# A router-driven expert loop on TensorE: the gate phase ahead of the down phase in each round

## The reference, cut to what matters

```python
def expert_block(args):                       # one block of up to 128 rows of one expert
    xblk, e = args
    gate = xblk @ w_gate[e] + b_gate[e]
    up = xblk @ w_up[e] + b_up[e]
    gate = jnp.minimum(gate, SWIGLU_LIMIT)
    up = jnp.clip(up, -SWIGLU_LIMIT, SWIGLU_LIMIT)
    h = (up + 1.0) * gate * jax.nn.sigmoid(SWIGLU_ALPHA * gate)
    return h @ w_down[e] + b_down[e]
```

## Time and profile before

| what | us |
|---|---|
| median of 3 runs (2397.16 to 2398.49) | 2397.28 |
| the profiled execution's own time | 2394.5 |
| its span in the profile | 2392.6 |
| TensorE matmuls busy (share of the span) | 2221.9 (93%) |
| VectorE busy | 1043.4 (44%) |
| ScalarE busy | 668.5 (28%) |
| GpSimd busy | 376.6 (16%) |

### The profile page before, as it was taken

One profiled execution on the slowest core, in us unless ns is written; L12 is line 12 of the kernel. 1 busy time (PEld: TensorE's weight loads), 2 busy tenths in 40 slices (PEclk: granted clock), 3 DMA queues, 4 the chain that ended last, 5 costly groups with the idle time before them and its releaser, 6 DMA issues.

```text
span 2392.6 us, 57077 instructions
## 1 busy us (share of the span) xinstructions
PE 2221.9 (93%) x21767; PEld 1176.8 (49%) x21768; DVE 1043.4 (44%) x1664; ACT 668.5 (28%) x1414; POOL 376.6 (16%) x491
## 2 busy tenths in 40 slices
PE   5999999998996599999999999999998999999982
PEld 3485765867454244545445454444443444444441
DVE  4154547445346344434434443443353444433334
ACT  5111222233344332222322222322232222222222
POOL 5000000000014212111111121111122112211111
PEclk9999999999997699999999999999999999999996
DMA  9112011126205294967979788888887897888864
GB/s 302 35 36 72 26 33 48 31 67 246 93 36 202 90 373 127 360 211 279 338 250 344 251 313 314 287 305 287 286 328 272 303 340 271 309 291 337 322 216 157
DMA packets 187702, 525.54 MB, mean 220 GB/s; under 512 B 20330, under 2 KB 68066, under 8 KB 187490
## 3 DMA queue, kind: packets, MB, share of 16 engines
q1 hardware_dynamic: 133874, 338.86, 37.7%
q10 hardware_dynamic: 36240, 134.29, 14.4%
q0 software_dynamic: 17536, 51.69, 9.6%
HBM read 486.21 MB, written 38.57 MB: 219 GB/s over the span
## 4 chain that ended last, share of the span: by engine, by line
PE 85%; DMA 6%; DVE 4%; issue 1%; ACT 1%; POOL 1%; ACTq 0%; SPq 0%; POOLq 0%; DVEq 0%
PE ps L1753 40%; PE ps L1786 19%; PE ps L1536 6%; PE ps L1637 5%; PE ps L1532 5%; DMA w_gu_e<-in_w_up_dram 4%; PE ps L1542 2%; PE ps L1593 2%; PE ps L1539 2%; PE ps L1615 1%; PE ps L1656 1%; PE ps L1508 1%; DMA w_down_e<-in_w_down_dram 1%; DVE box L1107 0%; DVE y_all L1460 0%
## 5 line engine op out<-in xcount | busy, mean ns | idle before, releaser
L1753 PE MATMUL ps<-w_gu_e,xT 128*32 128x512 f32 x9216 | 1007.7, 595 | 34.3 <-DVEq L1418 16.6
L1753 PEld LDWEIGHTS ps<-w_gu_e,xT 128*32 128x32 f32 x9216 | 355.9, 110 | 667.4 <-issue 667.1
L1786 PE MATMUL ps<-w_down_e,hT 128*32 128x256 f32 x9216 | 508.7, 380 | 13.4 <-ACT yrow L932 8.4
L1786 PEld LDWEIGHTS ps<-w_down_e,hT 128*32 128x32 f32 x9216 | 351.3, 110 | 181.8 <-issue 40.8
L1383 DVE STREAM_TRANSPOSE gu_t<-ps 128x1024 f32<-128x1024 f32 x94 | 111.9, 1229 | 639.4 <-PE ps L1753 639.4
L914 ACT ACTIVATE xT<-xr,fm 128x128 f32<-128x128 f32 x392 | 184.1, 490 | 569.0 <-PE ps L1753 544.6
L1369 DVE TENSOR_SCALAR yrow<-ps,slot_tab 32x256 f32<-32x256 f32 x376 | 181.3, 482 | 259.0 <-PE ps L1786 167.9
L932 ACT ACTIVATE yrow<-ps,slot_tab 32x256 f32<-32x256 f32 x384 | 179.4, 467 | 352.2 <-issue 235.9
L655 POOL DMA_INDIRECT xg<-xn_rows,idx_g x196 | 197.4, 1007 | 85.4 <-issue 47.6
L649 POOL TENSOR_TENSOR idx_g<-slot_tab,base_row 128x4 int32<-128x4 int32 x49 | 9.2, 189 | 1101.6 <-DVE xr L1405 1087.5
L1536 PE MATMUL ps<-hxT,w_ring 128*128 128x512 f32 (+1 forms) x384 | 142.5, 529 | 3.7 <-ACT hxT L802 3.7
(11 more groups left out here) (301 smaller groups left out, 1515.2 us busy)
## 6 DMA issues: line engine op xcount, KB each, us to landing
w_gu_e<-in_w_gate_dram SPq DMA_DIRECT2D x256, 512.0 KB, 10.7
w_gu_e<-in_w_up_dram SPq DMA_DIRECT2D x256, 512.0 KB, 11.6
w_down_e<-in_w_down_dram ACTq DMA_DIRECT2D x124, 1024.0 KB, 9.2
w_ring<-in_w_ada_dram SPq DMA_DIRECT2D x17, 1024.0 KB, 5.2
w_ring<-in_w_in_dram SPq DMA_DIRECT2D x20, 512.0 KB, 5.2
w_first<-in_w_ada_dram SPq DMA_DIRECT2D x7, 1024.0 KB, 12.2
x_all<-in_x_dram SPq DMA_DIRECT2D x2, 2048.0 KB, 10.6
w_out<-in_w_out_dram SPq DMA_DIRECT2D x8, 512.0 KB, 8.6
```

The lines of the kernel that those rows point to most:

```text
L1753: last = T.matmul(ps[j * GROUP:(j + 1) * GROUP, g, :].rearrange("p (w b f) -> p w b f", w=2, f=GROUP), xT[:, k, g * GROUP:(g + 1) * GROUP] ...
L1786: last = T.matmul(ps[j * GROUP:(j + 1) * GROUP, 4 + g // 2, g % 2 * QUARTER:(g % 2 + 1) * QUARTER], hT[:, g, k, :], w_dn[:, k, j * QUARTER ...
```

## The change

In TensorE's loop the gate phase of item n now stands ahead of the down phase, which is that of item n - 1, so there are n_items + 1 rounds and the packed table is shifted by one entry instead of two. The waits of the phases are renumbered by one and the increments that start the counts are moved to match: VectorE raises `yv_ready` once behind the tables and `hT_ready` behind the first item's rows. The gate phase's branch tree asks for size 1 first and has that body first in the code. The wait for the first rows' banks, ahead of the loop before, is now part of the gate phase's own wait: ScalarE raises `gu_evac` by 2 behind the first rows, and every wait on `gu_evac` counts 2 more.

```diff
@@ rounds, and ScalarE behind the first rows @@
-            return eng.value_load(int_n[0:1, 2:3], min_val=NE + 2, max_val=ITEMS + 2)
+            return eng.value_load(int_n[0:1, 2:3], min_val=NE + 1, max_val=ITEMS + 1)
...
             first_rows(4)
+            act.sem_inc(gu_evac, 2)
@@ VectorE: tables @@
-            for k, more in enumerate((-1.0, -2.0, 2.0)):
+            for k, more in enumerate((-1.0, -2.0, 1.0)):
...
-            V.tensor_copy(int_q[:, 0:2], tab_q[:, 0:2])
-            V.scalar_tensor_tensor(out=int_q[:, 2:NTAB], in0=tab_w[:, 0:NTAB - 2], scalar=8.0, in1=tab_q[:, 2:NTAB],
+            V.tensor_copy(int_q[:, 0:1], tab_q[:, 0:1])
+            V.scalar_tensor_tensor(out=int_q[:, 1:NTAB], in0=tab_w[:, 0:NTAB - 1], scalar=8.0, in1=tab_q[:, 1:NTAB],
                                    op0=ALU.mult, op1=ALU.add).then_inc(tables, 1)
             dve.wait_ge(tables, 1)
+            dve.sem_inc(yv_ready, 1)
...
-                dve.wait_ge(gu_evac, m * 2 + 2)
+                dve.wait_ge(gu_evac, m * 2 + 4)
...
             rows_turned(0)
+            dve.sem_inc(hT_ready, 1)
             rows_turned(1)
...
-            dve.sem_inc(hT_ready, 1)
-            dve.sem_inc(yv_ready, 2)
+            dve.sem_inc(yv_ready, 1)
             swiglu(0, link)
@@ TensorE @@
             def gate_up(m, loaded, size):
 
-                pe.wait_ge(gu_evac, m * 2)
+                pe.wait_ge(gu_evac, m * 2 + 2)
                 apart(pe)
-                with pe.If(size > 1):
-                    with pe.If(size > 2):
-                        with pe.If(size == 4):
-                            gate_up_of(m, loaded, (2, 3), False)
-                        with pe.Else():
-                            gate_up_of(m, loaded, (2,), False)
-                    gate_up_of(m, loaded, (0, 1), True)
+                with pe.If(size == 1):
+                    gate_up_of(m, loaded, (0,), True)
                 with pe.Else():
-                    with pe.If(size > 0):
-                        gate_up_of(m, loaded, (0,), True)
+                    with pe.If(size > 1):
+                        with pe.If(size > 2):
+                            with pe.If(size == 4):
+                                gate_up_of(m, loaded, (2, 3), False)
+                            with pe.Else():
+                                gate_up_of(m, loaded, (2,), False)
+                        gate_up_of(m, loaded, (0, 1), True)
                     with pe.Else():
                         pe.sem_inc(gu_used, KT)
...
-                pe.wait_ge(hT_ready, n)
-                pe.wait_ge(yr_ready, n)
-                pe.wait_ge(yv_ready, n)
+                pe.wait_ge(hT_ready, n + 1)
+                pe.wait_ge(yr_ready, n + 1)
+                pe.wait_ge(yv_ready, n + 1)
...
-            pe.wait_ge(y0_ready, 2 * TL)
             with pe.Fori(0, n_rounds) as n:
                 pair = item_pair(pe, n)
+                gate_up(n, ((pair >> 6) & 63) * 32, pair & 7)
                 down(n, (pair >> 12) * 16, (pair >> 3) & 7)
-                gate_up(n, ((pair >> 6) & 63) * 32, pair & 7)
```

## The result

The changed kernel takes 2456.26 us (median of 6 runs, 2453.77 to 2458.81) against 2397.22 us for the kernel before, measured beside it (6 runs). The ratio is 1.0244, with a 95% interval of 1.0231 to 1.0258: 59.0 us slower, where 52.3 had been forecast. The profiled execution has a span of 2455.1 us, 62.5 more than that of before.

A forecast was written before the change was run, and what follows sets the result against it. TensorE was taken to bound the expert loop. Added sequencer path of 65.5 us, less 11.2 in existing waits, gives +54.3; less 2.0 at the start, +52.3 on 2397.28, so 2449.6 us, range 2425 to 2472.

The forecast's parts named there:

- The boundary: Loop count, branch and table read, hidden between gate and down phase, would show in full between down and gate: 1.1 us.
- The new test: Ahead of gate phases of size 2 to 4, testing size 1 first adds a taken branch: 0.3 us each.
- `m * 2 + 2`: Ahead of the gate phase, this count instead of m * 2 costs one more register operation: 0.1 us.
- Taken up by waits that exist: In the loop, existing weight waits (7.0 us), waits after size-1 gate phases (4.0) and one down phase absorb 11.2 us.
- From G to D nothing is given back: Gate to down phase: the path gets 1.1 us shorter but was hidden already, so nothing is gained.
- The start: Before the loop's steady part: first gate phase 9.4 us earlier, second gains between 1.1 and 6.9, taken as 2 us.
- three long branches behind G0: The three first-pass jumps would come after the first gate phase instead of ahead of it, lasting 11.4 us at equal cost.
- Nothing lies behind this but the loop: After the second gate phase's start, the opening was to bring no further cost before the loop's ordinary rounds.
- hidden: Rival: queued matmuls at a down phase's end cover the new path, leaving only the start, 2390.4 to 2396.2 us; chance 0.06.
- partly hidden: Rival: down to gate phase costs 1.0 us a round or less, +29 us or less, 2426 us; chance 0.08.
- The granted clock: Rival: TensorE's gaps between down and gate phases lower its clock, +37 us more, 2487 us; chance 0.08.
- Instructions loaded each round: Rival: the loop no longer stays loaded, at least 3.2 us in each of 47 rounds, +150, 2600 us; chance 0.02.

The follow-up runs named there:

- the second pair: Profiles taken a second time of the kernel before and the unaltered changed kernel, on another chip: spans 2410.2 and 2462.4 us.
- after_again: The changed kernel, unaltered, run a second time on another chip: ratio 1.0222 to the kernel before.
- fields_ahead_in_after: The changed kernel with the old size tests, the next round's word read and its fields computed among the gate matmuls: ratio 0.9979 to the kernel before.
- old_tree_in_after: The changed kernel with the gate phase's old order of size tests: ratio 1.0118 to the kernel before.

## Why the prediction was right, and where not

The direction, the place and the mechanism were right, and the time, 2449.6, is 6.7 us under the measured 2456.3. That the number came so close is in part luck, as the last point says.

- **The boundary, 1.1 us.** Right. 1.2 us in the single lines; more than half of it, the read of the table, was taken out alone (idle 1.44 to 0.70 us) and put in alone (0.64 us).
- **The new test, 0.3 us.** Right: 0.27 us by the idle time when it is undone, 0.24 by the gap when it is put into the kernel before.
- **`m * 2 + 2`, 0.1 us.** Wrong: it is one FUSED_REGOPS of 42 ns (L1732) in the place of one ALU_OP. The idle time is 1.44 us, not 1.5. With size 1 it is 0.92, not 1.0. Over the 44 changes behind G2 the gaps grew by 60.5 us, where these terms gave 64.
- **Taken up by waits that exist, 11.2 us.** The named ones are right: the weight waits fell from 11.1 to 3.9 us (forecast 7.0), the down phase behind a gate phase of size 1 waits 0.49 instead of 1.40 us. In all, 60.5 of gaps became 46.2 us of loop, so 14.3 were taken up: 7.2 in weight waits, 3.4 in the four down phases behind a gate phase of size 1 (forecast 4.0), 0.2 in one more down phase, and about 0.25 us of matmul time for each of the seven weight waits that are gone. A down phase's wait for weights gives 1.1 back. The rest, 2.9 us, is clock, and was not foreseen. In the kernel before, four weight waits fall into one gate phase, and the granted clock goes to half behind them; in the changed kernel three do, and it stays at 1.00. The same 136 matmuls, before and then after, each with a stretch of it in the columns of the earlier trace rows:
```profile
1842.83 17.65 PE L1753 MATMUL ps<-w_gu_e,xT 128*32 128x512 f32 x136 [1.43 <-DMA w_gu_e<-in_w_up_dram]
1843.00:1848.00 5.00, 5.00 (x28) 1.23 (x27) 0.00 (x0) 0.00 (x0) 3.58 (x4) 0.50 0.23 67
```
```profile
1892.79 14.80 PE L1755 MATMUL ps<-w_gu_e,xT 128*32 128x512 f32 x136 [1.44 <-DMA w_gu_e<-in_w_up_dram]
1893.00:1898.00 5.00, 5.00 (x52) 1.79 (x48) 0.00 (x0) 0.98 (x2) 3.08 (x4) 1.00 0.31 78
```
  This depends on the execution: in the second pair both kernels have such a fall in that phase (0.54 from 1895 to 1900 us in `after_again`). There the loop is 40.5 us slower, not 46.2.
- **From G to D nothing is given back.** Right. Over the loop the starts of down phases come 3.7 us closer to the gate phases ahead of them (19.8 us in sum instead of 23.4), but 3.4 of them are the four places behind a gate phase of size 1; all others together have 0.2.
- **The start, -2.0 us.** Right as far as G1: G0 13.1 us behind the first rows (12.4 forecast), G1 33.4 (33.8), with three long branches behind G0, 10.6 us in all (11.4).
- **"Nothing lies behind this but the loop."** This is the step that failed: a second load of instructions had been put at nothing. D0 lies behind it, and its instructions were loaded again: a branch of 6.1 us, another 4.5 us inside D0, and half the clock for D0. It made +12.5 us. I had taken the jumps as a fixed set of three that only moves; the number of loads differs with the order of the code that is passed. The runs show what the stall goes with: in the changed kernel twice and in the one with the read moved it is there, with 38 packets of instructions; with the old tests in the new order, and with the new tests in the old order, it is not (33 and 35). Which block displaces which was not shown.
- **The two misses offset each other in part**: +12.5 at D0 not seen, and 8 us less in the loop (46.2, not 54.3). Without the stall, the forecast would have been off by 6 us to the other side; in the second pair, where the loop has 40.5, the two misses nearly cancel (52.2 us of span against 52.3 forecast). That is luck.

Of the rivals: hidden is refuted by the 43 waits; partly hidden is refuted as a size (1.44 us of 1.5), but true for the old place, which hid about half of a read that showed by 0.64 us at the other. The granted clock is 1.00 over the loop's stretch with its 1.4 us gaps. A mean over 1000 us also reads 1.00 with 5 us at half in it, as the kernel before shows; but no gate phase of the changed kernel's first profile is longer than its matmuls and weight waits make it. What came new is the stretch at half at D0, behind 4.48 us of idle time. Instructions loaded each round did not come, but a single such load, in the second round, did.

The Trainium skill ("Runtime: NRT & Kernel Launch", Instruction fetch mechanics) says that a taken branch to code outside a window of two pages forces a fetch. The four long branches fit this, and so do the 6 packets around the fourth. That only two pages are held does not agree: a page is a block of 256 instructions there, a round with two phases of size 4 passes 512 matmuls and as many weight loads, and yet later rounds of either kernel take 0.07 to 0.23 us for the same branches and load nothing.

## What to carry to other kernels

How much register and branch work a change of phase can hide is set by the phase that stands ahead of it: the same queue of matmuls lasts 2.2 us with 512 columns and 1.1 us with 256. Ask it for each of the two changes, with the path on it, before a loop is turned; or put the reads and the arithmetic for the next round among the matmuls of the longer phase, where the queue has time to fill again. With that done either order came out 0.2% under the kernel before. And when a loop's code is passed in another order, look at the first and also at the second round for long branches: a jump that moves can bring another with it.

## What the runs showed of the hardware that was not expected

- Register work in the middle of a gate phase (a read of 0.30 us and the field arithmetic) is hardly seen: 27.68 against 27.67 us.
- Nearly the same code needs 33, 35 or 38 packets of instructions, by the order of its parts. The 38 of the changed kernel come with 9.0 us of idle time and half the clock for about 10 us; the 35 of two variants come without a stall at D0.
- In the old order with the old tests, the three first-pass branches last 11.1 to 12.1 us together in the four profiles with the banks' wait ahead of the loop, and 13.4 to 14.5 in the three with it inside, where they begin earlier.
- Waits of up to 1.5 us with 8 matmuls between them were followed by half the clock for about 5 us in the kernel before; three such waits in the changed kernel's first profile and its 43 gaps of 1.4 us between whole phases were not.
- In one layout the second of the two long branches behind G0 did not come (`fields_ahead_in_after`; single lines from 793 to 825 us; they lasted 4.1 and 3.7 us in `old_tree_in_after`). There the profile names VectorE's transposes as what G1 waits for. A branch of 2.03 us came once instead, at 872.4 us, inside D1, where 0.60 us of it show:
```profile
L1794 PEldq COMPARE_BRANCH  x1: 3762/3762/3762, 810.9 to 810.9; - x1
...
L1802 PEldq COMPARE_BRANCH  x1: 228/228/228, 814.8 to 814.8; - x1
```
